# The bias of the differential prompt attention, added on VectorE or accumulated on TensorE

## Chip, cores and metric

The kernel runs on 1 core of one Trainium2 chip. The metric is the device time of one execution in microseconds (us). The kernel before takes 4555.41 us (median of 3 runs, 4538.9 to 4556.95).

## What is computed

A hybrid encoder step with two layers. Each layer normalises the tokens, multiplies by `w_in`, runs four mixers, multiplies by `w_out` and ends with a gated feed-forward block. All data is fp32. The part that the change touches is the differential attention of the 1024 prompt tokens (4 heads, 2 components of 32 columns each, queries in blocks of 128):

```python
def core(qb, qp):
    s = jnp.einsum('bqhcd,bkhcd->bchqk', qb, k_all).astype(f32) * scale
    bias = jnp.take(t5_table, _t5_bucket(kpos[None, :] - qp[:, None]), axis=0)
    s = s + jnp.transpose(bias, (2, 0, 1)).astype(f32)
    p = _masked_softmax(s, _chunk_mask(qp, kpos))
    w = p[:, 0] - lam * p[:, 1]
    return jnp.einsum('bhqk,bkhd->bqhd', w.astype(v_all.dtype), v_all)
```

Beyond a distance of 128 keys the bias of a head is a constant, and a constant drops out of the softmax. So the kernel keeps a bias block of 128 queries by 256 keys for each head, relative to that constant, with -1e30 where the mask closes.

## The kernel before

The program is a row of stages for each layer. A stage is a block of instruction streams, one for each engine, that order one another by semaphores, and the next stage begins behind a barrier of all engines. The prompt attention stage is one function, `prompt_attention` (L747), used twice in a layer: for the latent attention (MLA, `comps` = 1, `bias` = None) and for the differential attention (`comps` = 2, with the bias block `bias_p`, which a short stage before it loads from DRAM). In the trace the first works on tiles `mla_P`, `mla_PT`, the second on `diff_P`, `diff_PT`.

The stage walks over 32 units: 8 query blocks `i`, and 4 heads in each. A unit of block `i` has n = 128 (i + 1) keys. I write k = i + 1 for its number of key tiles of 128.

For each unit TensorE does three things. `scores(v)` (L778) makes the scores of both components. Component c writes to PSUM banks 0 and 1 or banks 2 and 3, in pieces of at most 512 columns. Its operands `dqT` and `dkT` stand on a strip of 32 partitions that differs between the components. `turn(v)` (L791) transposes the combined weights tile by tile, and `values(v)` (L800) multiplies them by the values. An fp32 product is two instructions in the trace (two passes), a transpose is one. TensorE's order is scores(v+1), values(v-1), turn(v), scores(v+2), and so on.

VectorE adds the bias to the last 256 columns of the scores (L825), waits for that to be written (`link`), and takes the row maximum (L826). It does so for component 0, then 1, of unit v+1 (`maxima`), and then combines the two components of unit v (L843), which `turn(v)` waits for. ScalarE does the two exponentials with their sums (L872), scales component 0 (L876) and copies the transposed weights (L858) and, once for a query block, the output (L862). `scores` of a component waits for the exponential of the unit before (`p_done`), which frees its PSUM banks.

Of the kernel before, what the change touches and what calls it, by code (L numbers as in the profile page):

```python
# [7 lines left out]
ALU = mybir.AluOpType  # L8
# [3 lines left out]
P = 128  # L12
# [86 lines left out]
def build(nc, d):  # L99
    top = ExitStack()  # L100
    with top:
# [56 lines left out]
        def C(name):  # L158
            return cst[:, CC[name][0]:CC[name][1]]
# [5 lines left out]
        def K8(name, rows, a=0, b=None):  # L165
            lo, hi = C8[name]
            rows = rows if isinstance(rows, slice) else slice(0, rows)
            return cst8[rows, lo + a:(hi if b is None else lo + b)]
# [578 lines left out]
        def prompt_attention(block, sems, comps, q_of, k_of, v_of, Pb, PTb, stat, bias, o_out, minus_lam=None):  # L747

            s_ready, max_done, p_done, r_ready, p_scaled, w_ready, pt_ready, pt_done, av_done, o_done, lnk = sems
            units = [(i, hh) for i in range(PT_TILES) for hh in range(HEADS)]
            U = len(units)

            def S(v, c):
                m = comps * v + c
                return PS[:, 2 * (m % 2):2 * (m % 2) + 2, :].rearrange("p a b -> p (a b)")

            PTP = PS[:, 4:6, :].rearrange("p a b -> p (a b)")

            def O(i, hh):
                return PS[64 * (hh % 2):64 * (hh % 2) + 64, 6 + i % 2, (hh // 2) * P:(hh // 2 + 1) * P]

            @block.tensor
            def _(pe):
                def scores(v):
                    i, hh = units[v]
                    n = P * (i + 1)  # L770
                    for c in range(comps):
                        m = comps * v + c
                        if m >= 2:
                            pe.wait_ge(p_done, m - 1)
                        for at in range(0, n, 512):
                            w = min(512, n - at)
                            masked = at + w == n and bias is None
                            mm = pe.matmul(S(v, c)[:, at:at + w], q_of(hh, c, i), k_of(hh, c, at, w), start=True,  # L778
                                           stop=not masked)
                        if bias is None:  # L780
                            mm = pe.matmul(S(v, c)[:, n - P:n], K8("first_half", 1), K8("second_half", 1),
                                           start=False, stop=True)
                        mm.then_inc(s_ready, 1)

                def turn(v):
                    i, hh = units[v]
                    pe.wait_ge(w_ready, v + 1)
                    if v >= 1:
                        pe.wait_ge(pt_done, v)
                    for t in range(i + 1):  # L790
                        mm = pe.transpose(PTP[:, t * P:(t + 1) * P], Pb[:, v % 2, 0, t * P:(t + 1) * P], C("ident"))  # L791
                    mm.then_inc(pt_ready, 1)

                def values(v):
                    i, hh = units[v]
                    pe.wait_ge(pt_done, v + 1)
                    if hh == 0 and i >= 2:
                        pe.wait_ge(o_done, i - 1)
                    for t in range(i + 1):
                        mm = pe.matmul(O(i, hh), v_of(hh, t), PTb[:, v % 2, t * P:(t + 1) * P],  # L800
                                       start=(t == 0), stop=(t == i))
                    mm.then_inc(av_done, 1)

                scores(0)
                for v in range(U):
                    if v + 1 < U:
                        scores(v + 1)
                    if v >= 1:
                        values(v - 1)
                    turn(v)  # L810
                values(U - 1)

            @block.vector
            def _(dve):
                link = Link(dve, lnk)

                def maxima(v):
                    i, hh = units[v]
                    n = P * (i + 1)
                    for c in range(comps):  # L820
                        dve.wait_ge(s_ready, comps * v + c + 1)
                        if bias is not None:
                            w = min(n, 256)
                            near = S(v, c)[:, n - w:n]
                            link(dve.tensor_tensor(near, near, bias(hh)[:, 256 - w:256], ALU.add))  # L825
                        dve.tensor_reduce(stat[:, 0, v, c:c + 1], S(v, c)[:, 0:n], AX_X, ALU.max,  # L826
                                          negate=True).then_inc(max_done, 1)

                maxima(0)
                for v in range(U):  # L830
                    i, hh = units[v]
                    n = P * (i + 1)
                    dve.wait_ge(p_done, comps * (v + 1))
                    rec = dve.reciprocal(stat[:, 2, v, :], stat[:, 1, v, :])
                    if comps == 2:
                        link(rec)
                        rec = dve.tensor_scalar(stat[:, 2, v, 1:2], stat[:, 2, v, 1:2], minus_lam, None, ALU.mult)
                    rec.then_inc(r_ready, 1)
                    if v + 1 < U:
                        maxima(v + 1)  # L840
                    if comps == 2:
                        dve.wait_ge(p_scaled, v + 1)
                        dve.scalar_tensor_tensor(out=Pb[:, v % 2, 0, 0:n], in0=Pb[:, v % 2, 1, 0:n],  # L843
                                                 scalar=stat[:, 2, v, 1:2], in1=Pb[:, v % 2, 0, 0:n],
                                                 op0=ALU.mult, op1=ALU.add).then_inc(w_ready, 1)
                    else:
                        dve.wait_ge(r_ready, v + 1)
                        dve.tensor_scalar(Pb[:, v % 2, 0, 0:n], Pb[:, v % 2, 0, 0:n], stat[:, 2, v, 0:1], None,
                                          ALU.mult).then_inc(w_ready, 1)

            @block.scalar
            def _(act):
                def copy_turned(v):
                    i, hh = units[v]
                    act.wait_ge(pt_ready, v + 1)
                    if v >= 2:
                        act.wait_ge(av_done, v - 1)
                    act.copy(PTb[:, v % 2, 0:P * (i + 1)], PTP[:, 0:P * (i + 1)]).then_inc(pt_done, 1)  # L858

                def copy_out(i):  # L860
                    act.wait_ge(av_done, HEADS * (i + 1))
                    act.copy(o_out[:, :, i * P:(i + 1) * P],  # L862
                             PS[:, 6 + i % 2, 0:256].rearrange("p (t q) -> p t q", t=2)).then_inc(o_done, 1)

                for v in range(U):
                    i, hh = units[v]
                    n = P * (i + 1)
                    for c in range(comps):
                        act.wait_ge(max_done, comps * v + c + 1)
                        if v >= 2 and c == 0:  # L870
                            act.wait_ge(pt_ready, v - 1)
                        act.activation(Pb[:, v % 2, c, 0:n], S(v, c)[:, 0:n], ACT.Exp, bias=stat[:, 0, v, c:c + 1],  # L872
                                       accum_out=stat[:, 1, v, c:c + 1]).then_inc(p_done, 1)
                    if comps == 2:
                        act.wait_ge(r_ready, v + 1)
                        act.mul(Pb[:, v % 2, 0, 0:n], Pb[:, v % 2, 0, 0:n], stat[:, 2, v, 0:1]).then_inc(p_scaled, 1)  # L876
                    if v >= 1:
                        copy_turned(v - 1)
                    if hh == 2 and i >= 1:
                        copy_out(i - 1)  # L880
                copy_turned(U - 1)
                copy_out(PT_TILES - 1)
# [1412 lines left out]
```

## Time and profile before

| | us |
|---|---|
| median of 3 runs | 4555.41 (4538.9 to 4556.95) |
| the profiled execution | 4543.31 |
| its span in the profile | 4541.5 |
| TensorE matmul busy | 3969.9 (87%) |
| VectorE busy | 1926.3 (42%) |
| ScalarE busy | 1141.1 (25%) |
| GpSimd busy | 790.9 (17%) |

The granted TensorE clock is 0.874 of full speed over the span. The full speed is 2.4 GHz, the other level, shown as 0.50, is 1.2 GHz. Read the shares with care: the stages have different limits, and a busy TensorE at half clock does half the work.

### The profile page before, as it was taken

The page shows a single profiled execution, that of the slowest core. Times are in us where ns is not written, and L with a number is a line of the kernel's source. Part 1 is how long each engine was busy: PE and PEld are TensorE (multiplying, and loading weights), DVE is VectorE, ACT ScalarE, POOL GpSimd, SP SyncE. Part 2 cuts the span into 40 slices and gives each one's busy share as a digit, 9 for nine tenths or more (in the row PEclk, how much of TensorE's full clock was granted, in tenths as well). Part 3 has the DMA queues.
Part 4 walks back from the last instruction along what each step waited for, and adds up shares of the span by engine and source line. Part 5 has one row for each costly group of instructions (what it writes and reads, how often), then busy time and mean ns, then how long its engine had stood idle before and what let it go on. Part 6 is the DMA issues. An engine that isn't in the chain of part 4 may idle for free. (4 is left out here: it accounts for less than half of the span.)

```text
span 4541.5 us, 52320 instructions
## 1 busy us (share of the span) xinstructions
PE 3969.9 (87%) x21722; PEld 3520.7 (78%) x21722; DVE 1926.3 (42%) x3051; ACT 1141.1 (25%) x2055; POOL 790.9 (17%) x622
## 2 busy tenths in 40 slices
PE   4999878789798999999879998768897799999996
PEld 2998535559588999999869975445896799999995
DVE  3521335255424445444453222443553344445444
ACT  2222324123213121212132132441331222121211
POOL 1211000001113222322122100000111223222320
PEclk8999955579799999999989987565898899999998
DMA  4121000010011111111022110000101011111111
GB/s 149 53 71 49 22 7 1 37 57 1 21 33 36 42 38 38 42 42 38 23 108 74 44 35 22 7 34 4 58 2 39 27 38 42 42 38 38 42 42 46
DMA packets 48415, 179.72 MB, mean 40 GB/s; under 512 B 13828, under 2 KB 16388, under 8 KB 44776
## 3 DMA queue, kind: packets, MB, share of 16 engines
q1 hardware_dynamic: 48168, 176.27, 11.7%
q8 instruction: 174, 2.85, 0.3%
q14 instruction: 73, 0.60, 0.0%
HBM read 148.04 MB, written 28.22 MB: 39 GB/s over the span
## 5 line engine op out<-in xcount | busy, mean ns | idle before, releaser
L238 PE MATMUL PS<-h_split,w_split 128*128 128x384 f32 x3072 | 1042.8, 339 | 48.4 <-PEq L178 48.4
L240 PE MATMUL PS<-h_split,w_split 128*128 128x384 f32 x3072 | 1041.2, 339 | 0.0
L239 PE MATMUL PS<-h_split,w_split 128*128 128x384 f32 x3072 | 1036.9, 338 | 0.0
L233 POOL TENSOR_TENSOR w_split<-w_full,w_split 128x1024 fp32r<-128x1024 f32 (+1 forms) x196 | 497.5, 2539 | 1088.7 <-ACT w_split L225 1086.6
L238 PEld LDWEIGHTS PS<-h_split,w_split 128*128 128x128 f32 x3072 | 585.8, 191 | 51.2 <-issue 51.2
L239 PEld LDWEIGHTS PS<-h_split,w_split 128*128 128x128 f32 x3072 | 578.8, 188 | 0.6 <-issue 0.6
L240 PEld LDWEIGHTS PS<-h_split,w_split 128*128 128x128 f32 x3072 | 579.2, 189 | 0.0
L225 ACT CAST w_split<-w_full 128x1024 fp32r<-128x1024 f32 (+1 forms) x196 | 204.4, 1055 | 912.0 <-PE PS L240 758.7
L238 PE MATMUL PS<-ffn_act,w_split 128*128 128x384 f32 x1056 | 367.2, 348 | 71.7 <-DVE x L1741 54.4
L1741 DVE TENSOR_TENSOR x<-x,PS 128x384 f32<-128x384 f32 x528 | 287.0, 552 | 235.2 <-PE PS L240 234.9
L239 PE MATMUL PS<-ffn_act,w_split 128*128 128x384 f32 x1056 | 364.9, 346 | 0.0
L240 PE MATMUL PS<-ffn_act,w_split 128*128 128x384 f32 x1056 | 364.1, 345 | 0.0
L238 PEld LDWEIGHTS PS<-ffn_act,w_split 128*128 128x128 f32 x1056 | 206.5, 196 | 78.7 <-DVE x L1741 60.9
L1749 DVE TENSOR_SCALAR ffn_up<-ffn_row,par 128x1168 f32<-128x1168 f32 x44 | 36.7, 835 | 465.9 <-ACT ffn_row L1726 465.9
L239 PEld LDWEIGHTS PS<-ffn_act,w_split 128*128 128x128 f32 x1056 | 205.8, 195 | 0.0
L240 PEld LDWEIGHTS PS<-ffn_act,w_split 128*128 128x128 f32 x1056 | 205.3, 194 | 0.0
L1200 POOL MEMSET q_decayed<- 128x1536 f32 x2 | 2.8, 1377 | 1064.6 <-POOLq L178 1064.6
L238 PE MATMUL PS<-o_hi,w_split 128*128 128x384 f32 x384 | 131.9, 344 | 30.0 <-DVE o_lo L1567 30.0
L778 PE MATMUL PS<-dkT,dqT 32*128 32x512 f32 (+3 forms) x384 | 133.9, 817 | 13.6 <-PEq L178 11.3
L800 PEld LDWEIGHTS PS<-diff_PT,dv 128*64 128x64 f32 x576 | 101.4, 204 | 56.6 <-issue 31.0
L791 PE MATMUL PS<-cst,diff_P 128*128 128x128 f32 x288 | 68.5, 388 | 84.4 <-DVE diff_P L843 84.4
L872 ACT ACTIVATE diff_P<-PS,diff_stat 128x256 f32<-128x256 f32 (+7 forms) x128 | 94.8, 741 | 188.7 <-DVE diff_stat L826 187.8
(329 smaller groups left out, 6132.1 us busy)
## 6 DMA issues: line engine op xcount, KB each, us to landing
w_full<-in_w_up SPq DMA_DIRECT2D x88, 512.0 KB, 3.5
w_full<-in_w_down SPq DMA_DIRECT2D x44, 512.0 KB, 3.5
w_full<-in_w_in SPq DMA_DIRECT2D x40, 512.0 KB, 3.6
x_keep<-x SPq DMA_DIRECT2D x2, 4608.0 KB, 19.7
x<-x_keep SPq DMA_DIRECT2D x2, 4608.0 KB, 15.0
w_full<-in_w_out SPq DMA_DIRECT2D x16, 512.0 KB, 3.6
x<-in_xT SPq DMA_DIRECT2D x1, 4608.0 KB, 16.0
out_o_y<-yT SPq DMA_DIRECT2D x1, 4608.0 KB, 12.3
```

The lines of the kernel that those rows point to most:

```text
L225: act.copy(ws[:, n % SSLOTS, 0, 0:w], wf[:, n % WSLOTS, 0:w]).then_inc(w_hid, 1)
L233: pool.tensor_tensor(ws[:, n % SSLOTS, 1, 0:w], wf[:, n % WSLOTS, 0:w], ws[:, n % SSLOTS, 0, 0:w].bitcast(F32), ALU.subtract).then_inc(w_l ...
L238: pe.matmul(out, w_hi, a_hi, start=first, stop=False)
L239: pe.matmul(out, w_hi, a_lo, start=False, stop=False)
L240: return pe.matmul(out, w_lo, a_hi, start=False, stop=last)
L778: mm = pe.matmul(S(v, c)[:, at:at + w], q_of(hh, c, i), k_of(hh, c, at, w), start=True, stop=not masked)
L791: mm = pe.transpose(PTP[:, t * P:(t + 1) * P], Pb[:, v % 2, 0, t * P:(t + 1) * P], C("ident"))
L800: mm = pe.matmul(O(i, hh), v_of(hh, t), PTb[:, v % 2, t * P:(t + 1) * P], start=(t == 0), stop=(t == i))
L872: act.activation(Pb[:, v % 2, c, 0:n], S(v, c)[:, 0:n], ACT.Exp, bias=stat[:, 0, v, c:c + 1], accum_out=stat[:, 1, v, c:c + 1]).then_inc(p ...
L1200: pool.memset(qd[:, :, :, :, :], 0.0)
L1741: dve.tensor_tensor(xs, xs, PS[:, 4 + u % 4, 0:BLK], ALU.add).then_inc(added, 1)
L1749: link(dve.tensor_scalar(acc[:, 0:L], row[:, 0:L], w(0), None, ALU.mult))
```

## The change

The addition on VectorE is taken out. In `scores`, each piece of a component's scores that overlaps the last 256 columns is followed by a second product into the same PSUM columns: the 128 by 128 identity as the stationary operand, the bias block as the moving one, accumulated (`start=False`). Where the last 256 columns straddle two pieces (n = 640) there are two such products of 128 columns, with n = 128 there is one of 128 columns, else one of 256. The MLA attention keeps its mask product.

```diff
                         for at in range(0, n, 512):
                             w = min(512, n - at)
-                            masked = at + w == n and bias is None
+                            lo = max(at, n - (P if bias is None else 256))
+                            near = slice(lo, at + w)
+                            added = lo < at + w
                             mm = pe.matmul(S(v, c)[:, at:at + w], q_of(hh, c, i), k_of(hh, c, at, w), start=True,
-                                           stop=not masked)
-                        if bias is None:
-                            mm = pe.matmul(S(v, c)[:, n - P:n], K8("first_half", 1), K8("second_half", 1),
-                                           start=False, stop=True)
+                                           stop=not added)
+                            if added and bias is None:
+                                mm = pe.matmul(S(v, c)[:, near], K8("first_half", 1), K8("second_half", 1),
+                                               start=False, stop=True)
+                            elif added:
+                                mm = pe.matmul(S(v, c)[:, near], C("ident"),
+                                               bias(hh)[:, 256 - n + lo:256 - n + at + w], start=False, stop=True)
                         mm.then_inc(s_ready, 1)
...
                         dve.wait_ge(s_ready, comps * v + c + 1)
-                        if bias is not None:
-                            w = min(n, 256)
-                            near = S(v, c)[:, n - w:n]
-                            link(dve.tensor_tensor(near, near, bias(hh)[:, 256 - w:256], ALU.add))
                         dve.tensor_reduce(stat[:, 0, v, c:c + 1], S(v, c)[:, 0:n], AX_X, ALU.max,
```

## Rows read from the trace of the kernel before

**Rows 1.** Who waited for whom, 620 to 818 us: waiting, releaser, us, times, longest.

```profile
ACT diff_P L872 <- DVE diff_stat L826: 95.9, 59, 12.0
DVE PS L825 <- PE PS L778: 85.6, 31, 6.1
PE PS L791 <- DVE diff_P L843: 41.7, 31, 2.7
```

**Rows 2.** Timeline, all engines, one unit with k = 5 (start us, us, engine).

```profile
699.87 0.43 DVE L825 TENSOR_TENSOR PS<-PS,bias_p 128x256 f32<-128x256 f32 x1 [2.93 <-PE PS L778]
700.34 0.82 DVE L826 TENSOR_REDUCE diff_stat<-PS 128x1 f32<-128x640 f32 x1
701.08 0.42 DVE L825 TENSOR_TENSOR PS<-PS,bias_p 128x256 f32<-128x256 f32 x1
701.53 0.82 DVE L826 TENSOR_REDUCE diff_stat<-PS 128x1 f32<-128x640 f32 x1
702.27 0.88 DVE L843 SCALAR_TENSOR_TENSOR diff_P<-diff_P,diff_stat 128x640 f32<-128x640 f32 x1
703.20 1.33 PE L791 MATMUL PS<-cst,diff_P 128*128 128x128 f32 x5 [1.46 <-DVE diff_P L843]
704.46 2.51 PE L778 MATMUL PS<-dkT,dqT 32*128 32x512 f32 x8
706.90 2.39 PE L800 MATMUL PS<-diff_PT,dv 128*64 128x128 f32 x10
707.00 0.43 DVE L825 TENSOR_TENSOR PS<-PS,bias_p 128x256 f32<-128x256 f32 x1 [3.27 <-PE PS L778]
```

**Rows 3.** Timeline of TensorE, a unit with k = 8 at full clock.

```profile
799.38 1.09 PE L791 MATMUL PS<-cst,diff_P 128*128 128x128 f32 x8 [1.85 <-DVE diff_P L843]
800.40 1.99 PE L778 MATMUL PS<-dkT,dqT 32*128 32x512 f32 x8
802.33 1.96 PE L800 MATMUL PS<-diff_PT,dv 128*64 128x128 f32 x16
```

**Rows 4.** Timeline, MLA samples: products of 128, 32, 128 rows into one region.

```profile
602.00 1.11 PE L1807 MATMUL PS<-kT,q_lat 128*64 128x256 f32 x2
603.04 0.69 PE L1808 MATMUL PS<-krT,q_rope 32*64 32x128 f32 x2
603.66 0.69 PE L1809 MATMUL PS<-latT,q_lat 128*64 128x128 f32 x2
```

**Rows 5.** Groups of VectorE by shape, 620 to 829 us: busy us, mean ns.

```profile
L826 DVE TENSOR_REDUCE diff_stat<-PS 128x1 f32<-128x128 f32 x8 | 2.3, 291 | 0.3
L826 DVE TENSOR_REDUCE diff_stat<-PS 128x1 f32<-128x1024 f32 x8 | 9.8, 1224 | 0.3
L843 DVE SCALAR_TENSOR_TENSOR diff_P<-diff_P,diff_stat 128x128 f32<-128x128 f32 x4 | 1.4, 342 | 0.0
L843 DVE SCALAR_TENSOR_TENSOR diff_P<-diff_P,diff_stat 128x1024 f32<-128x1024 f32 x4 | 5.1, 1277 | 1.2 <-ACT diff_P L876 1.2
```

**Rows 6.** Timeline: first scores and last output copy of the stage, both layers.

```profile
620.88 0.80 PE L778 MATMUL PS<-dkT,dqT 32*128 32x128 f32 x4 [5.76 <-PEq L178]
828.14 0.37 ACT L862 COPY o_diff<-PS 128x256 f32<-128x256 f32 x1 [2.05 <-PE PS L800]
2850.37 0.79 PE L778 MATMUL PS<-dkT,dqT 32*128 32x128 f32 x4 [5.54 <-PEq L178]
3053.71 0.37 ACT L862 COPY o_diff<-PS 128x256 f32<-128x256 f32 x1 [2.05 <-PE PS L800]
```

**Rows 7.** Windows: us, busy us (instructions) by engine, granted clock, DMA share, GB/s.

```profile
440.00:464.00 24.00, 23.75 (x69) 13.68 (x68) 6.80 (x23) 7.46 (x24) 0.00 (x0) 0.50 0.00 1
500.00:556.00 56.00, 51.68 (x312) 36.38 (x313) 21.17 (x34) 23.89 (x37) 0.00 (x0) 1.00 0.00 1
620.80:749.00 128.20, 99.98 (x344) 58.61 (x344) 68.84 (x165) 59.87 (x145) 0.00 (x0) 0.50 0.00 1
749.00:829.00 80.00, 62.03 (x280) 41.97 (x280) 38.67 (x60) 38.39 (x56) 0.00 (x0) 0.70 0.00 0
2849.40:2961.00 111.60, 85.38 (x292) 49.09 (x292) 59.72 (x150) 51.37 (x130) 0.00 (x0) 0.50 0.00 1
2961.00:3055.00 94.00, 71.71 (x334) 48.64 (x332) 48.02 (x77) 46.65 (x71) 0.00 (x0) 0.73 0.00 1
```

## What I predicted, and how I came to it

> **What bounds the stage now.** I read the two executions of the stage first: from the first scores to the end of the last output copy they take 207.6 us and 203.7 us, 411 of the 4541.5 us of the span [rows 6]. Nothing outside them is touched, so only these 411 us matter. I then read the list of waits. VectorE waits 85.6 us for TensorE's scores, and TensorE waits 41.7 us for VectorE's combination [rows 1]. Two engines that wait for each other in turn form a loop, and neither is the bound alone.
>
> The timeline of one unit with k = 5 shows the loop [rows 2]. VectorE adds and reduces component 0 (699.87 to 701.08), adds and reduces component 1 (to 702.27) and combines. TensorE then turns at 703.20, and makes the next scores at 704.46. These end at 706.97, and the next addition starts at 707.00. One round is 7.13 us: 3.33 us from the first addition to the start of the turning, 3.80 us of TensorE up to the next addition. The values (2.39 us from 706.90) lie beside VectorE's work and set nothing, since TensorE then idles for over 1 us. So both halves of the edit fall on the path: what VectorE loses is a gain in full, what TensorE gets in `scores` is a loss in full.
>
> The granted clock was 0.50 (1.2 GHz) for the first 128 us and a mean of 0.70 for the last 80 us in the first layer. In the second layer it was 0.50 for 112 us and then 0.73 for 94 us [rows 7]. That is some 15 to 20% of the stage at full clock. This decides what a product costs.
>
> **Prices of TensorE, from rows.** A pass over 128 columns costs 0.213 us at half clock: 10 passes of the values took 2.39 us, and a first one alone would be 0.475 [rows 2]. At full clock 16 passes took 1.96 us, and 15 steps of 0.109 us with a first of 0.32 us make that up [rows 3]. An fp32 product has two passes, so 0.427 us or 0.214 us for 128 columns.
>
> The eight score instructions of k = 5 are 2 components times 2 passes times 640 columns, 20 passes over 128 columns. One after another they would be 20 x 0.213 = 4.27 us, but they took 2.51 us. Ten passes and a first latency of 0.38 us are 2.51 us. So the two components, which stand on different strips of 32 partitions, run side by side in the array. At full clock it is the same: 1.99 us for 32 passes, which one by one would be 3.4 us [rows 3].
>
> **What the change adds.** Each component gets a bias product of 2 passes over 256 columns: 0.853 us at half clock, 0.43 us at full clock (half of it for k = 1). It uses all 128 rows. In the trace there is no such product between two score products. The nearest rows are the sample stage, where products of 128, 32 and 128 rows follow one another in one sum. None overlaps there: two passes over 256 columns are 0.853 us, and the next one, with 32 rows, starts after 1.04 us; its own two passes are 0.427 us, and the next starts after 0.62 us [rows 4]. So they run in order, and each change between row heights costs 0.19 us more. With the wide stationary operand of this stage the turning (5 passes, 1.07 us) is followed by scores after 1.26 us, and the scores (10 passes side by side, 2.13 us) by the values after 2.44 us [rows 2]. Those are changes of 0.19 us and 0.31 us.
>
> I therefore expect the order to become: scores of c0, bias, scores of c1, bias, one after another. The side by side run is lost, which costs 0.427 k us at half clock. A unit then has four changes of height, where it had two. I take the dearer 0.30 us each, as the identity is 128 columns wide; with 0.19 us it would be 0.4 us less for each unit. For k = 5, where the bias straddles two pieces, there are eight. At full clock the four changes are 0.8 us (in rows 3 the two make 0.39 us).
>
> The Trainium skill has a rule that speaks against this change. In the page "TensorEngine Tiling (Array Packing)", section "Key Properties", it says that a change of the tiling mode (not just of the tile) drains the engine, and that different tiles can work in parallel. By it the 128-row identity between the 32-row strips ends the parallel run, as rows 4 lead one to expect.
>
> **What it removes.** 128 additions of 0.43 us. From start to start each costs VectorE 0.47 and 0.45 us (699.87 to 700.34, 701.08 to 701.53), so 0.92 us for each unit [rows 2]. Beyond that, with the scores in series, c0's maximum is taken while c1's scores run. For k = 5 that takes another 0.74 us off the loop. The exponentials stay hidden. The wait of `scores` for `p_done` is not made longer, as the second exponential ends long before TensorE's turn is over. No DMA and nothing on GpSimd or SyncE moves.
>
> **The new round at half clock.** TensorE's own work is: turn 0.213 k, scores 0.853 k, two biases 1.71, values 0.427 k, changes 1.2, that is 1.493 k + 2.9 us. The chain through VectorE is: turn, scores, biases and changes (1.066 k + 2.9), 0.25 us of latency, then one maximum and the combination. The maximum is 0.29 us for 128 columns and 1.22 us for 1024, the combination 0.34 and 1.28 us [rows 5], together 0.37 + 0.267 k. That makes 1.33 k + 3.5 us. The longer of both counts, and TensorE becomes the bound from k = 4. For k = 1 to 8 I get 4.0, 6.2, 7.5, 8.9, 11.6 (with its four extra changes), 11.9, 13.4 and 14.8 us, 78.3 in all. Four heads make 313 us, and some 5 us for the end of the stage make 318 us. For k = 5 it is 11.6 us against 7.13 now.
>
> **The new round at full clock.** The chain is 0.107 k + 0.427 k + 0.85 + 0.8 + 0.2 of latency + 0.37 + 0.267 k, or 0.80 k + 2.25 us. Over all units that is 187 us, with the end 192 us. This is 14 us less than the mean of now (206 us, mostly at half clock).
>
> **How much of it runs at full clock.** This is the uncertain term. Against a high share: the stage starts at 1.2 GHz, and its scores fill a quarter of the rows. The MLA stage, whose scores have 96 rows, stayed at 0.50 in 440 to 464 us with TensorE busy for 23.75 of 24 us, and came to 1.00 only later [rows 7]. For a high share: TensorE loses its idle time, its work of full height (turn, values, and now bias) is in one piece between c1's and c0's scores, and MLA, once up, stayed up with 51.7 of 56 us busy [rows 7]. The share of time with full height is 45% for k = 5 at half clock, before (3.2 of 7.1 us) and after (4.9 of 11.6, and 42%). I expect patches of full clock again, more of them than the 15 to 20% of now and fewer than MLA's: 40% of the time. The stage then takes 1 / (0.6/318 + 0.4/192) = 252 us. A share of 0.2 gives 280 us, one of 0.6 gives 228 us.
>
> **Sum.** 252 - 206 = 46 us for each layer, 93 us for both. On the profiled execution (4543.3 us) that is 4636 us. That execution lies 12 us below the median of the three runs, which themselves span 18 us, so from the median it would be 4648 us. I take 4642 us.
>
> **Rivals.** (1) The full clock carries it, and the time is not slower. If the identity products keep TensorE dense enough for 2.4 GHz nearly all through, as in MLA, the stage takes 192 us and the kernel 4555 - 28 = 4527 us. It decides at a full-clock share of some 0.83, where 1 / (0.17/318 + 0.83/192) = 206 us. For it: TensorE never waits at k above 3, and MLA does it. Against it: half of TensorE's time is quarter height, and now the clock fell back again and again after 749 us.
>
> (2) The clock stays down for nearly all of the stage. Then it takes 300 to 318 us, and the kernel 4555 + 2 x 103 = 4761 us. For it: scores in series are longer stretches of quarter height than any now, up to 3.4 us each at k = 8. Against it: the clock rises now with less work of full height.
>
> (3) The change doesn't do to the array what I say: c1's scores still run beside c0's, and the biases alone follow. Then a unit gets 1.71 + 0.6 us and loses 0.92 us at half clock, and at full clock 0.85 + 0.4 against 0.92. With 64 units, four fifths of them at half clock, that is 64 x (0.8 x 1.39 + 0.2 x 0.33) = 75 us, or 58 us with changes of 0.19 us. The kernel takes 4613 to 4630 us. Rows 4 speak against it.
>
> **Chances.** The forecast has 0.70, rival 1 has 0.10, rival 2 has 0.10 and rival 3 has 0.10. A measurement of this kernel can tell about 0.5% (23 us) from no change. Within the forecast the share of full clock runs from 0.15 to 0.8, which is 290 to 209 us for a stage, or 4561 to 4723 us. Hence slower by over 0.5% has 0.84, within 0.5% has 0.09 (high shares of full clock), faster by over 0.5% has 0.07. The range of 4565 to 4735 us leaves out rival 1, most of rival 2 and a little of the forecast.
>
> **What would show it.** The scores of c0 and c1 (L778) start apart by more than the length of c0's, with products of `cst` and `bias_p` between them. For k = 4 the two components with their biases take about 6.0 us at half clock (3.4 + 1.7 + 0.9 for three changes). TensorE's idle time before L791 falls from 41.7 us to under 15 us. The row for L825 is gone, and VectorE's wait for scores grows from 85.6 us. The stage takes about 250 us, with a mean clock near 0.7. I am wrong if c1's scores still start beside c0's (rival 3), or if the mean clock of the stage is over 0.9 or under 0.55.

## The result, and the profile after

The changed kernel takes 4645.08 us (median of 4 runs, 4643.15 to 4670.44) against 4549.13 us before (median of 4 runs; the 4555.41 us above was the median of the first three). The ratio, estimated from all runs and not from the two medians, is 1.0225, with a 95% interval of 1.02 to 1.0251. The changed kernel is slower by 96 us.

First the windows of the two stages in the changed kernel (columns as in rows 7), from the first scores to the end of the last output copy:

```profile
620.70:892.90 272.20, 265.86 (x768) 145.65 (x768) 83.99 (x160) 98.83 (x200) 0.00 (x0) 0.63 0.00 0
2912.70:3160.10 247.40, 236.87 (x768) 128.64 (x768) 83.96 (x160) 97.91 (x200) 0.00 (x0) 0.72 0.00 0
```

Before, the two took 207.6 and 203.7 us [rows 6]. They are longer by 64.6 and 43.7 us, 108 us together, while the span grew by 102.9 us (4541.5 to 4644.4). The remaining 5 us lie outside the two stages, where nothing was edited. In the profiled executions of the experiments below, the time outside the stages goes from 4131 to 4143 us, so it varies by more than that. The mean clock did not fall, it rose: 0.63 and 0.72, against 0.58 and 0.60 over the same stages before:

```profile
620.80:828.50 207.70, 162.00 (x624) 100.58 (x624) 107.51 (x224) 98.25 (x200) 0.00 (x0) 0.58 0.00 1
2850.30:3054.10 203.80, 157.08 (x624) 97.73 (x624) 107.50 (x224) 98.02 (x200) 0.00 (x0) 0.60 0.00 1
```

TensorE is now busy for 266 of 272 us.

The waits of the first stage, the counterpart of rows 1 (waiting, releaser, us, times, longest):

```profile
DVE diff_stat L827 <- PE PS L786: 178.2, 64, 6.6
ACT diff_P L873 <- DVE diff_stat L827: 157.2, 63, 12.2
PE PS L796 <- DVE diff_P L844: 3.2, 6, 0.8
```

The loop of two engines is gone. VectorE waits twice as long as before, now for the bias product (L786), and 64 times instead of 31, once for each component. TensorE's wait for the combination fell from 41.7 to 3.2 us. TensorE is the bound.

TensorE's timeline for a unit with k = 4 at half clock, the counterpart of rows 2:

```profile
706.80 1.12 PE L796 MATMUL PS<-cst,diff_P 128*128 128x128 f32 x4
707.85 2.07 PE L780 MATMUL PS<-dkT,dqT 32*128 32x512 f32 x2
709.85 1.22 PE L786 MATMUL PS<-bias_p,cst 128*128 128x256 f32 x2
711.00 2.07 PE L780 MATMUL PS<-dkT,dqT 32*128 32x512 f32 x2
713.00 1.22 PE L786 MATMUL PS<-bias_p,cst 128*128 128x256 f32 x2
714.15 1.97 PE L805 MATMUL PS<-diff_PT,dv 128*64 128x128 f32 x8
```

Read it by the starts (c0 and c1 are components 0 and 1). The scores of c0 take 2.00 us to the next start, of which two passes over 512 columns are 1.71. The bias takes 1.15 us, of which its passes are 0.85. Then the same again for c1. So each of these four steps costs 0.29 to 0.30 us beyond its passes, and nothing overlaps. Three of the steps change the row height. The fourth, from c1's bias to the values, keeps 128 rows and changes only the width of the stationary operand, from 128 to 64 columns. Two more steps cost less: from the turning to the scores 0.20 us, which is a change of height, and from the values to the next turning (at 716.05 us) 0.19 us, which is none. What costs time is thus a change in the shape of the operands, and the height is only one part of that shape. In rows 2 the same line L778 handled both components in 2.51 us for k = 5.

### The profile page after: what moved, and what is told of

Read it like the earlier page. It is cut to its first block and busy times, and to the rows that moved or that the text cites. A ratio compares the mean times of both kernels' runs of the same rounds, so it can differ in the third digit from the quotient of the medians.

```text
span 4644.4 us, 52768 instructions
## 1 busy us (share of the span) xinstructions
PE 4149.0 (89%) x22010; PEld 3593.0 (77%) x22010; DVE 1879.3 (40%) x2923; ACT 1141.8 (25%) x2055; POOL 791.2 (17%) x622
## 3 DMA queue, kind: packets, MB, share of 16 engines
q1 hardware_dynamic: 48168, 176.27, 11.3%
## 5 line engine op out<-in xcount | busy, mean ns | idle before, releaser
L827 DVE TENSOR_REDUCE diff_stat<-PS 128x1 f32<-128x256 f32 (+7 forms) x128 | 97.0, 758 | 331.6 <-PE PS L786 331.6
L780 PE MATMUL PS<-dkT,dqT 32*128 32x512 f32 (+3 forms) x384 | 220.9, 686 | 11.2 <-PEq L178 11.2
L786 PEld LDWEIGHTS PS<-bias_p,cst 128*128 128x128 f32 x288 | 62.9, 272 | 106.3 <-issue 105.8
```

The source lines that it names most:

```text
L786: mm = pe.matmul(S(v, c)[:, near], C("ident"), bias(hh)[:, 256 - n + lo:256 - n + at + w], start=False, stop=True)
```

## Experiments

All times are medians. Times of the stage are of the profiled execution, for the first and the second layer.

**e1: both scores, then both biases.**

```diff
                         for at in range(0, n, 512):
                             w = min(512, n - at)
-                            lo = max(at, n - (P if bias is None else 256))
-                            near = slice(lo, at + w)
-                            added = lo < at + w
                             mm = pe.matmul(S(v, c)[:, at:at + w], q_of(hh, c, i), k_of(hh, c, at, w), start=True,
-                                           stop=not added)
+                                           stop=at + w <= n - (P if bias is None else 256))
+                    for c in range(comps):
+                        for at in range(0, n, 512):
+                            w = min(512, n - at)
+                            lo = max(at, n - (P if bias is None else 256))
+                            near = slice(lo, at + w)
+                            if lo >= at + w:
+                                continue
...
                         mm.then_inc(s_ready, 1)
```

> The scores of both components are issued first and then both bias products, so the two score products can run side by side again and each unit changes row height twice instead of four times (eight at k = 5); the bias stays on TensorE. My theory (most of the loss is the lost side by side run and the height changes, and the clock follows TensorE's full-height work): at half clock a unit loses 0.427 k + 0.6 us against the changed kernel, the stage takes about 172 us a layer with more full clock than before, the kernel about 4549 - 66 = 4485 us. Rival (the bias products' own streaming, 1.7 us a unit at half clock, is the loss): the stage stays over 230 us and the kernel over 4600 us.

Measured: 4473.27 us against 4554.83 us before on the same chip, a ratio of 0.9834 (0.9813 to 0.9855). The windows of its two stages, and TensorE's timeline of units with k = 5 at full clock:

```profile
623.50:790.50 167.00, 139.60 (x768) 90.31 (x768) 81.74 (x160) 94.49 (x200) 0.00 (x0) 0.92 0.00 1
2815.90:2983.20 167.30, 140.77 (x768) 91.14 (x768) 81.73 (x160) 94.49 (x200) 0.00 (x0) 0.91 0.00 1
```

```profile
698.64 0.76 PE L800 MATMUL PS<-cst,diff_P 128*128 128x128 f32 x5 [0.76 <-DVE diff_P L848]
699.33 1.35 PE L777 MATMUL PS<-dkT,dqT 32*128 32x512 f32 x8
700.62 1.16 PE L790 MATMUL PS<-bias_p,cst 128*128 128x128 f32 x8
701.71 1.31 PE L809 MATMUL PS<-diff_PT,dv 128*64 128x128 f32 x10
703.77 0.77 PE L800 MATMUL PS<-cst,diff_P 128*128 128x128 f32 x5 [0.76 <-DVE diff_P L848]
```

The eight score instructions take 1.35 us again (side by side), a round is 5.1 us, and the clock stays at 1.00 for most of the stage. In the time as a whole the bias product itself is not the loss: all of it is still on TensorE here, and this version beats both kernels. How much of the gain is the order and how much the clock is read below, from rounds at one clock.

**e2: no bias at all.**

```diff
-                        if bias is not None:
-                            w = min(n, 256)
-                            near = S(v, c)[:, n - w:n]
-                            link(dve.tensor_tensor(near, near, bias(hh)[:, 256 - w:256], ALU.add))
```

> The kernel before without the addition and without the product: the bias (and with it the mask inside it) is left out. Shows what VectorE's additions cost on the path. 0.92 us a unit at half clock is 29 us a layer; with the denser TensorE also more full clock. I expect 161 to 176 us a layer and 4460 to 4490 us. If VectorE's additions were off the path, it would stay at 4549 us.

Measured: 4468.45 us, ratio 0.9814 (0.9783 to 0.9845). Windows of the stages:

```profile
624.50:794.30 169.80, 147.45 (x624) 91.44 (x624) 81.08 (x160) 94.19 (x200) 0.00 (x0) 0.65 0.00 1
2819.60:2979.60 160.00, 135.25 (x624) 83.96 (x624) 81.08 (x160) 94.05 (x200) 0.00 (x0) 0.71 0.00 1
```

VectorE's additions were on the path: without them a layer takes about 165 us instead of 206. Of these 41 us, 29 us are the additions at the price of rows 2, and the clock rose from 0.59 to 0.68 besides. The trace bears the price out: at half clock the start of one turning follows the last by 6.20 us for k = 5, against 7.13 us before. e1, which computes the bias, is within 5 us of this kernel, which doesn't.

**e3: the changed order with a bias of 32 columns** (most of the bias is left out).

```diff
-                            lo = max(at, n - (P if bias is None else 256))
+                            lo = max(at, n - (P if bias is None else 32))
```

> The changed kernel with the bias product cut to the last 32 columns, so that its streaming is an eighth (most of the bias is left out) while the order of products and the height changes stay. Theory (series and height changes are the larger part): 224 us a layer, about 4585 us. Rival (streaming of the bias is the loss): about the time without any bias, under 4500 us.

Measured: 4617.28 us, ratio 1.0141 (1.0121 to 1.0161), 32 us more than my theory gave. One thing besides the columns differs from the changed kernel: for k = 5 the bias of 32 columns no longer straddles two pieces, so these units have four changes of height and not eight. Windows of the stages, and one bias product with what follows it:

```profile
621.70:868.20 246.50, 242.07 (x752) 148.36 (x752) 83.99 (x160) 99.06 (x200) 0.00 (x0) 0.60 0.00 0
2892.70:3136.70 244.00, 238.37 (x752) 146.49 (x752) 83.98 (x160) 98.86 (x200) 0.00 (x0) 0.61 0.00 1
```

```profile
700.46 0.64 PE L786 MATMUL PS<-bias_p,cst 128*128 128x32 f32 x2
701.02 1.97 PE L805 MATMUL PS<-diff_PT,dv 128*64 128x128 f32 x8
```

An eighth of the columns still costs 0.56 us from start to start, against 1.15 us for the whole bias. So about half of a bias product's place in this order stays when its columns go. Even with hardly any bias, this order takes 245 us a layer against 165 in e2, in part by a lower clock (0.60 and 0.61 against 0.65 and 0.71). The clock is also lower than in the changed kernel (0.63 and 0.72), which may be part of why the smaller bias saved only 28 us against 4645 us.

**e4: the kernel before with superfluous work.**

```diff
+                    for _ in range(4 if comps == 2 else 0):
+                        pe.matmul(O(i, hh), v_of(hh, 0), PTb[:, v % 2, 0:P], start=True, stop=True)
                     for t in range(i + 1):
```

> The kernel before with four superfluous full-height products of 128 columns ahead of the values of each differential unit, overwritten by the real ones: 1.7 us of extra TensorE work a unit at half clock, put where TensorE waits for VectorE. Theory (the clock follows TensorE's full-height work, and the stage is slow because it runs at 1.2 GHz): mean granted clock of the stage about 0.9, 176 us a layer, about 4490 us, faster than before although it does more. Rival (the clock doesn't follow): the mean clock stays at 0.6, 210 to 220 us a layer and 4555 to 4580 us.

Measured: 4488.23 us, ratio 0.9861 (0.9843 to 0.988). Windows of the stages:

```profile
624.30:798.40 174.10, 136.37 (x880) 98.17 (x880) 107.55 (x224) 97.46 (x200) 0.00 (x0) 0.92 0.00 1
2823.60:2996.80 173.20, 134.46 (x880) 96.51 (x880) 107.53 (x224) 97.40 (x200) 0.00 (x0) 0.94 0.00 1
```

The kernel does 256 more products and is 67 us faster, since the clock went from 0.59 to 0.93. All that was changed is how densely TensorE works at full height while VectorE holds it up. At full clock the superfluous products cost nothing: a round of the loop with k = 6 takes 6.13 us in both kernels. This shows that the slow stage before was in good part a matter of the clock.

**e5: the kernel before, both components on one strip** (component 1 is left out).

```diff
-                r = 32 * (2 * (hh % 2) + c)
+                r = 32 * (2 * (hh % 2))
```

> The kernel before with both components read from the strip of component 0 (component 1 is left out: it repeats component 0), so that the two score products cannot run side by side; no height change and no bias product is added. It prices the lost side by side run alone. TensorE gets 0.427 k us more a unit at half clock, but component 0's addition and maximum then lie beside component 1's scores. My theory has the series cost 27 us a layer at a steady half clock and nothing at full clock, about 207 us a layer with the clock's share as it comes, so 4550 to 4600 us; the height changes and the bias's streaming must then hold the rest of the changed kernel's loss. Rival (the lost side by side run is the whole loss): 250 us a layer, 4640 us.

Measured: 4550.87 us against 4547.78 us, ratio 1.0005 (0.999 to 1.002): no difference. Windows of the stages:

```profile
622.40:828.20 205.80, 191.82 (x624) 116.07 (x624) 109.55 (x224) 98.09 (x200) 0.00 (x0) 0.64 0.00 1
2851.10:3056.40 205.30, 190.26 (x624) 116.18 (x624) 109.48 (x224) 97.91 (x200) 0.00 (x0) 0.64 0.00 1
```

TensorE is busy for 191 us a layer instead of 160, so the side by side run is gone, and yet the stage is as long as before. c0's addition and maximum now lie beside c1's scores, and the clock is a little higher (0.64 against 0.59). In the kernel before, the loss that I put first does not show in the time. This is the sum of two effects and not a price of nothing: at half clock a round with k = 4 takes 6.73 us here against 6.09 us before, and the higher clock gave that back.

**e6: the changed kernel with the superfluous work of e4.**

```diff
+                    for _ in range(4 if comps == 2 else 0):
+                        pe.matmul(O(i, hh), v_of(hh, 0), PTb[:, v % 2, 0:P], start=True, stop=True)
                     for t in range(i + 1):
```

> The changed kernel with four superfluous full-height products of 128 columns ahead of the values of each differential unit, overwritten by the real ones. At one clock this can only cost. Theory (much of the changed kernel's loss is that it runs at 1.2 GHz for most of the stage): the full clock's share rises to about 0.7 of the time, 228 us a layer instead of 260, about 4580 us. Rival (the clock is not moved by it, or the stage is bound by TensorE at either clock): 1.7 us a unit more at half clock, about 4645 + 80 = 4725 us.

Measured: 4584.99 us, ratio 1.0101 (1.0062 to 1.014) to before. Windows of the stages:

```profile
623.20:845.50 222.30, 219.02 (x1024) 138.45 (x1024) 83.99 (x160) 98.06 (x200) 0.00 (x0) 0.91 0.00 1
2866.90:3091.60 224.70, 221.46 (x1024) 140.55 (x1024) 83.97 (x160) 98.27 (x200) 0.00 (x0) 0.90 0.00 1
```

More work on the engine that is the bound, and 60 us less time. So the changed kernel runs most of its stage at 1.2 GHz, and this costs it at least the 36 us a layer that e6 is shorter. It is not what sets it apart from the kernel before, whose clock was lower still. Even at 0.90 the stage takes 223 us, 50 us more than e4 with the same superfluous work and about the same clock (0.93). Those 50 us are what the change costs at that clock: the bias products and their order, less the additions that fell away.

**e7: the order of e1, both components on one strip** (component 1 is left out). The edit is e1's and e5's together.

> The grouped order of e1 (scores, scores, bias, bias), with both components read from component 0's strip, so that the scores cannot run side by side (component 1 is left out: it repeats component 0). Against e1 it prices the series with the bias on TensorE, against the changed kernel it prices the two extra height changes and c0's earlier start. In the kernel before the series alone cost nothing, as component 0's addition and maximum then lay beside component 1's scores; here no addition is left to hide. My theory: 222 us a layer (212 to 233) against 167 in e1, about 4580 us. Rival (the series costs nothing here either, only the height changes do): about 170 us a layer, 4480 us.

Measured: 4563.02 us, ratio 1.0032 (1.002 to 1.0044) to before. Windows of the stages:

```profile
624.10:837.80 213.70, 196.11 (x768) 123.35 (x768) 82.12 (x160) 95.47 (x200) 0.00 (x0) 0.81 0.00 1
2859.70:3076.00 216.30, 202.50 (x768) 129.07 (x768) 82.20 (x160) 95.72 (x200) 0.00 (x0) 0.78 0.00 1
```

Against e1 the series costs 90 us in all, 48 us a layer, with the clock at 0.80 instead of 0.92. Against the changed kernel, which has the same products in series, two more changes of height a unit and six more at k = 5, it is 82 us shorter, 45 us a layer, with the clock at 0.80 instead of 0.67. Both differences include the clock's answer.

**The same kernels at one clock.** The traces hold rounds that ran at a single clock throughout. A round is taken from the start of one turning to the start of the next, in us, where turning, scores and values have the same k. The clock is the granted one over that round.

| | k = 1, 0.50 | k = 2, 0.50 | k = 4, 0.50 | k = 6, 1.00 | k = 7, 1.00 |
|---|---|---|---|---|---|
| before | 2.70 | 4.01 | 6.09 | 6.13 | 6.86 |
| changed | 4.01 | 6.26 | 9.25 | 7.07 | 7.88 |
| e1, grouped | 3.00 | 4.83 | | 5.84 | 6.56 |
| e4, before + 4 | | | | 6.13 | 6.86 |
| e5, before, one strip | 2.71 | 4.07 | 6.73 | | 6.89 |
| e7, grouped, one strip | 3.42 | 5.67 | | 7.12 | 8.06 |

The turnings of the rounds with k = 6, of the kernel before, the changed kernel and e1:

```profile
2969.39 0.87 PE L791 MATMUL PS<-cst,diff_P 128*128 128x128 f32 x6 [1.23 <-DVE diff_P L843]
2975.53 0.87 PE L791 MATMUL PS<-cst,diff_P 128*128 128x128 f32 x6 [2.31 <-DVE diff_P L843]
3067.05 0.88 PE L796 MATMUL PS<-cst,diff_P 128*128 128x128 f32 x6 [0.74 <-DVE diff_P L844]
3074.12 0.88 PE L796 MATMUL PS<-cst,diff_P 128*128 128x128 f32 x6 [0.52 <-DVE diff_P L844]
720.95 0.87 PE L800 MATMUL PS<-cst,diff_P 128*128 128x128 f32 x6 [0.96 <-DVE diff_P L848]
726.79 0.87 PE L800 MATMUL PS<-cst,diff_P 128*128 128x128 f32 x6 [0.95 <-DVE diff_P L848]
```

The changed kernel loses at either clock: 1.31 to 3.16 us a unit at half clock, about 1 us at full clock. The split of the half-clock loss for k = 2 (2.25 us) is 0.84 us for the series (e7 less e1), 0.59 us for the two extra changes of height (changed less e7), and 0.82 us for the bias products less the additions (e1 less before). The first is 0.427 k and the second 2 x 0.30 us, as the prediction had them. At full clock the series costs 1.28 us for k = 6, but the two extra changes cost nothing (7.07 against 7.12 us).

Grouping alone does not make the change a gain. At half clock e1 is 0.30 and 0.82 us a unit longer than the kernel before, at full clock 0.3 us shorter. Over 32 units this 0.3 us is 10 us a layer at most, by estimate, and e1 gained 39. So most of its gain over the kernel before came with the clock, which was 0.92 instead of 0.59.

## Why the prediction was right, step by step

**The forecast.** 4642 us was predicted, 4645 us measured. This closeness is partly luck. By its own steps the sum for the profiled execution was +93 us from the stages. They grew by 108 us, and 5 us came back elsewhere. The 4642 us was then put between two starting points, 4636 and 4648 us. From the median before, the forecast was +87 us, and +96 us was measured.

**The prices held.** For k = 4 I put the two components with their biases at 6.0 us with three changes of height. The trace has 707.85 to 714.15, 6.30 us, in which the fourth step is that from the bias to the values. For k = 5 I gave 11.6 us a round. The turn at 733.73 is followed by the next at 745.02 us, 11.3 us:

```profile
733.73 1.12 PE L796 MATMUL PS<-cst,diff_P 128*128 128x128 f32 x4
745.02 1.27 PE L796 MATMUL PS<-cst,diff_P 128*128 128x128 f32 x5
```

Only the scores in between have k = 5 there. A whole round with k = 5 (turns at 754.08 and 766.01 us) takes 11.93 us. The full-clock rounds held best: by 0.80 k + 2.25 us they are 7.05 and 7.85 us for k = 6 and 7, measured 7.07 and 7.88. At half clock the sum was short. For k = 1 to 5 it gave 4.0, 6.2, 7.5, 8.9 and 11.6 us, measured 4.01, 6.26, 7.76, 9.25 and 11.93. From k = 3 between 0.26 and 0.35 us are missing. I had put the steps from bias to values and from values to turning at nothing, as they change no height, and they cost 0.30 and 0.19 us, while the one from turning to scores costs 0.20 and not 0.30.

**The order held.** The components no longer run side by side in the changed kernel, so rival 3 is out. (Its own sum had a slip: with changes of 0.19 us it gives 64 us and not 58.) The Trainium skill, in the page "TensorEngine Tiling (Array Packing)", section "Key Properties", says that a change of the tiling mode, that is of how the array is divided, drains TensorE. The trace agrees in so far as a change costs time: the four steps above, where the shape changes, cost 0.29 to 0.30 us each. In e7, where c1's scores follow c0's in the same shape, four passes over 256 columns (1.71 us) take 2.00 us up to the bias, so there is one such cost and not two:

```profile
648.05 2.07 PE L777 MATMUL PS<-dkT,dqT 32*128 32x256 f32 x4
650.05 2.08 PE L790 MATMUL PS<-bias_p,cst 128*128 128x256 f32 x4
```

**The clock's share was the term that was off.** I took 0.40 of the time at full clock. The mean clocks of 0.63 and 0.72 are shares of 0.26 and 0.44. The two ends that I had worked out, 318 us at half and 192 us at full clock, join them well: 1 / (0.74/318 + 0.26/192) = 272 us, measured 272.2, and 1 / (0.56/318 + 0.44/192) = 247 us, measured 247.4. A part of this is luck, since the time missing in each round put the half-clock end some 9 us too low (an estimate); with 327 us the same sums give 277 and 250 us. The same program gave two shares in its two layers. So the share is not a constant of the code alone, and my single value could only be right on the mean, which was 0.35.

**Rival 1 failed, and the trace fits the reason given.** The clock fell back during the quarter-height scores again and again: in the changed kernel it fell 16 times in the two stages, and in 15 of them scores were running. One such fall lies in c1's scores of a unit with k = 5. The bias product ahead of them takes 0.49 us, the one behind them, of the same shape, 0.80 us:

```profile
748.11 0.49 PE L786 MATMUL PS<-bias_p,cst 128*128 128x128 f32 x2
748.53 1.12 PE L780 MATMUL PS<-dkT,dqT 32*128 32x512 f32 x2
749.58 0.80 PE L786 MATMUL PS<-bias_p,cst 128*128 128x128 f32 x2
```

Whether it was the height of the scores that made it fall was not isolated. e6 reached 0.90 with more full-height work, but even there the stage was 223 us and not below 206, in part since the superfluous work was itself on the path (7.36 us a round against 7.07 for k = 6 at full clock). Rival 2 failed too: the clock was higher than before, not lower.

**What I had in the wrong place.** The text named the lost side by side run first, at 0.427 k us a unit. e5 shows that in the kernel before this alone does not show in the time, and e7 that it costs 48 us a layer once the bias is on TensorE. The price was right as TensorE's own time, as the rounds of e7 and e1 show; whether it reaches the time depends on what else the loop holds and on the clock. And I did not see that the same edit with another order would gain. By my own numbers, two changes of height fewer and scores side by side take 0.427 k + 0.6 us off the round at half clock. That alone would not have made it faster than before: at half clock the rounds of e1 are still the longer ones. The clock did the rest, and no sum of mine foresaw how much.

## What to carry to other kernels

Products that use few rows of the array and run side by side on different strips are broken up by a full-height product put between them. Group them: all small ones, then all full-height ones (here 4645 us became 4473 us). Before moving work from VectorE to TensorE, count the changes of operand shape that it adds and look at the granted clock of the stage. In a stage at half clock a TensorE that is made denser can win more than it is given to do, as in e4 and e6. And before a gain or a loss is put down to the order of instructions, compare rounds that ran at the same clock: next to the kernel before, a round of e1 is longer at half clock and shorter at full clock.

## What the runs showed of the hardware

Superfluous work made two kernels faster. 256 extra products took the kernel before from 4555 to 4488 us, and the changed one from 4645 to 4585 us, with the clock of the stages going from 0.59 to 0.93 and from 0.67 to 0.90. How busy TensorE was does not sort these clocks: e3 had it busy for 98% of its first stage at 0.60, e4 for 78% at 0.92. The runs do not isolate which property of the products does.

The array starts a later product ahead of an earlier one, if they stand on different strips. In the kernel before, c1's scores come behind all pieces of c0 in the program. For k = 5 its timeline of TensorE has these, in two narrow windows (704.4 to 704.6 us, and 706.0 to 706.4 us):

```profile
704.46 1.23 PE L778 MATMUL PS<-dkT,dqT 32*128 32x512 f32 x2
705.48 1.28 PE L778 MATMUL PS<-dkT,dqT 32*128 32x512 f32 x4
```

Two passes start at 704.46 us and both end within 1.23 us, while two such passes one after the other take 2.07 us (at 707.85 us in the changed kernel). The next pass starts only at 705.48 us. So the pair at 704.46 us is the first pass of each component, and c1's ran ahead of c0's second.

A change in the shape of the operands costs time even where the number of rows stays: 0.30 us at half clock from the 128-column bias product to the 64-column values, as much as from 32 rows to 128.

A full-height product of 32 columns takes 0.56 us of TensorE at half clock in this order, half of one with 256 columns (1.15 us).
